# Token compression of a hybrid decoder step: cache pages laid by fours over the partitions, and turned in 32 x 32 blocks by VectorE

## What is computed

```python
CMP_BLOCK = 32; CMP_STRIDE = 16; CMP_HID = 256
def compress_rows(rows, pe, w1, w2):
    chunks = rows.reshape(B, nch, CMP_STRIDE, NSA_GROUPS, NSA_DK)
    w1r = w1.reshape(R, CMP_STRIDE, NSA_DK, CMP_HID)      # R = 2
    h = jnp.einsum('ld,ldh->h', pe, w1.reshape(CMP_BLOCK, NSA_DK, CMP_HID))
    for r in range(R):
        part = jnp.einsum('bcjgd,jdh->bcgh', chunks, w1r[r])
        h = h + part[:, r:r + nc]
    return jnp.einsum('bcgh,hd->bcgd', jax.nn.gelu(h), w2)
```

## Time and profile before

| | us |
|---|---|
| median of 3 runs | 1766.05 |
| lowest and highest | 1763.57, 1773.09 |
| the profiled execution | 1772.42 |
| its span | 1770.6 |
| compression stage in it | 413 to 681 |
| granted clock of TensorE, mean | 0.953 |

### The profile page before, as it was taken

How to read it: one execution, slowest core, us unless ns; L and a number is a source line. 1 busy time by engine, 2 the same in 40 slices (tenths; PEclk the granted TensorE clock), 3 DMA queues, 4 the chain that set the end, 5 groups by cost and what they waited for, 6 DMA issues and landing times. The chain is left out here.

```text
span 1770.6 us, 32705 instructions
## 1 busy us (share of the span) xinstructions
PE 1653.9 (93%) x12968; PEld 1374.8 (78%) x12968; DVE 804.5 (45%) x1873; ACT 585.9 (33%) x1235; POOL 105.8 (6%) x194
## 2 busy tenths in 40 slices
PE   6999999998799997789999989998979999999997
PEld 4888888776688885567677766766767999999997
DVE  4576543124233335866765643553554442234322
ACT  4232212222233234655554422332433331123210
POOL 0000000000000000034421200000010000000000
PEclk9999999999899998989897989999989999999999
DMA  8845545342533035531331089999752243333321
GB/s 276 296 163 165 157 160 164 97 131 57 139 72 77 7 98 153 138 137 58 109 110 36 7 315 369 363 371 346 278 177 72 95 129 113 113 113 124 96 71 51
DMA packets 187903, 265.71 MB, mean 150 GB/s; under 512 B 35261, under 2 KB 115517, under 8 KB 187654
## 3 DMA queue, kind: packets, MB, share of 16 engines
q1 hardware_dynamic: 183750, 244.31, 42.8%
q10 hardware_dynamic: 3136, 11.22, 1.7%
q0 software_dynamic: 896, 8.56, 1.5%
HBM read 240.98 MB, written 42.60 MB: 160 GB/s over the span
## 5 line engine op out<-in xcount | busy, mean ns | idle before, releaser
L620 PE MATMUL pj_ps<-all_hi,pj_xh 128*128 128x512 f32 x480 | 192.0, 400 | 1.5 <-DVE all_lo L509 1.5
L621 PE MATMUL pj_ps<-all_lo,pj_xh 128*128 128x512 f32 x480 | 190.0, 396 | 0.0
L622 PE MATMUL pj_ps<-all_hi,pj_xl 128*128 128x512 f32 x480 | 189.9, 396 | 0.0
L1431 ACT ACTIVATE pa_sc<-pa_sc,pa_nmax 128x32 f32<-128x32 f32 (+4 forms) x256 | 126.0, 493 | 124.9 <-DVE pa_nmax L1480 124.5
L2687 PE MATMUL fi_ps<-fi_fl,fi_wh 128*128 128x272 f32 x512 | 149.4, 292 | 0.0
L2688 PE MATMUL fi_ps<-fi_th,fi_wl 128*128 128x272 f32 x512 | 148.3, 290 | 0.0
L2688 PE MATMUL fi_ps<-fi_fh,fi_wl 128*128 128x272 f32 x512 | 148.3, 290 | 0.0
L2686 PE MATMUL fi_ps<-fi_th,fi_wh 128*128 128x272 f32 x512 | 147.6, 288 | 0.7 <-DVE fi_tl L2488 0.7
L2686 PE MATMUL fi_ps<-fi_fh,fi_wh 128*128 128x272 f32 x512 | 148.2, 290 | 0.0
L2687 PE MATMUL fi_ps<-fi_tl,fi_wh 128*128 128x272 f32 x512 | 147.2, 287 | 0.0
L2071 ACT ACTIVATE de_slot<-de_ps_t 128x512 f32<-128x512 f32 (+5 forms) x124 | 62.7, 513 | 174.8 <-PE de_ps_t L1905 85.3
(11 more groups left out here) (325 smaller groups left out, 3263.0 us busy)
## 6 DMA issues: line engine op xcount, KB each, us to landing
de_dv<-in_cache_diff SPq DMA_DIRECT2D x64, 512.0 KB, 10.1
all_big<-in_w_in SPq DMA_DIRECT2D x14, 2048.0 KB, 8.6
all_big<-in_cache_nsa SPq DMA_DIRECT2D x96, 256.0 KB, 5.9
de_dk<-in_cache_diff SPq DMA_DIRECT2D x48, 512.0 KB, 8.8
all_big<-in_w_up SPq DMA_DIRECT2D x16, 1024.0 KB, 5.5
all_big<-in_w_down SPq DMA_DIRECT2D x16, 1024.0 KB, 6.1
all_first<-in_cache_nsa SPq DMA_DIRECT2D x32, 256.0 KB
all_win<-in_cache_win SPq DMA_DIRECT2D x32, 256.0 KB, 7.2
```

Source lines behind the costliest of these rows:

```text
L620: pe.matmul(ps[:, t, :], xh[:, k, xk], hi(k), start=k == 0, stop=False)
L621: pe.matmul(ps[:, t, :], xh[:, k, xk], lo(k), start=False, stop=False)
L622: ins = pe.matmul(ps[:, t, :], xl[:, k, xk], hi(k), start=False, stop=k == KT - 1)
L1431: nc.scalar.activation(tile, tile, ACT.Exp, scale=-1.0, bias=nmax[:, x.n % 6, a:a + 1], accum_out=x.sums[a]).then_inc(probs, 1)
```

## The change

A quarter of the partitions now holds every fourth token. `page_load` issues four DMAs for a page, one for each remainder a of the token number by four: eight chunks of four tokens, to the partitions 32 a + 8 (i mod 4) + chunk, four tokens one behind the other at block i // 4 of the row. The rows of w1 and of the position embedding are laid in the matching order, each with eight DMAs of 32 partitions in place of one of 128. `lay_out` becomes two transposes on VectorE, each of 32 x 32 blocks over 128 partitions and 1024 elements, from the raw pages to `laid`, which is now in SBUF what `pt` was in PSUM. `high_parts` and `low_parts` read `laid`, in two pieces of 1024 elements in place of four of 512. TensorE's turns are gone. Chunks of one sequence now stand in order, so the second read of `xh` is one column on instead of 16, the copies behind the 128 columns are replaced by two columns of zeros set once, and a store is one DMA of 128 rows instead of eight.

```diff
-def page_load(nc, sp, g, d, dst, pair, i):
+def page_load(nc, sp, g, d, dst, pair, i, arrived):
 
     page = sp.value_load(g.table[0:1, PAGES_AT_ONCE * pair + i:PAGES_AT_ONCE * pair + i + 1],
                          min_val=0, max_val=d["cache_nsa"].shape[0] - 1)
-    chunks = d["cache_nsa"].rearrange("n (c j) e -> n c j e", j=CMP_STRIDE)
-    return sp.dma_start(dst[i:P:PAGES_AT_ONCE, :, :],
-                        chunks[bass.ds(page, 1), :, :, 0:2 * KVW].rearrange("n c j e -> (n c) j e"))
+    tokens = d["cache_nsa"].rearrange("n (c s a) e -> n a c s e", s=4, a=4)
+    block, at = divmod(i, 4)
+    for a in range(4):
+        rows = slice(32 * a + CHUNKS_PER_PAGE * at, 32 * a + CHUNKS_PER_PAGE * (at + 1))
+        sp.dma_start(dst[rows, 4 * block:4 * block + 4, :], tokens[bass.ds(page, 1), a, :, :, 0:2 * KVW]
+                     .rearrange("n c s e -> (n c) s e")).then_inc(arrived, 16)
+
+
+def turned_blocks(dst):
+
+    return dst.rearrange("p h g (b r) -> p b g h r", r=32)
...
-                    sp.dma_start(shared.big[:, 1 - k, :].rearrange("p (k n) -> p k n", n=CMP_HID),
-                                 d[f"cmp_w1_{'kv'[k]}"].rearrange("(k p) n -> p k n", p=P)).then_inc(shared.w1_in[k], 16)
+                    w1 = d[f"cmp_w1_{'kv'[k]}"].rearrange("(q a h i) n -> a h i q n", a=4, h=2, i=32)
+                    for a in range(4):
+                        for h in range(2):
+                            sp.dma_start(shared.big[32 * a:32 * a + 32, 1 - k, :].rearrange("p (q h n) -> p h q n", h=2, n=CMP_HID)
+                                         [:, h, :, :], w1[a, h, :, :, :]).then_inc(shared.w1_in[k], 16)
...
-            dve.wait_ge(shared.pages_in, 16 * PAGES_AT_ONCE)
-            first = shared.first[:].rearrange("p (j e) -> p j e", j=CMP_STRIDE)
-            nc.vector.tensor_copy(shared.laid[:].rearrange("p g (j e) -> p g j e", e=DK),
-                                  first[:, 0:JP, 0:KVW].rearrange("p j (g e) -> p g j e", e=DK)).then_inc(shared.laid_ahead, 1)
+            dve.wait_ge(shared.pages_in, 64 * PAGES_AT_ONCE)
+            first = shared.first[:].rearrange("p (b s e) -> p b s e", b=4, s=4)
+            for s2 in range(2):
+                nc.vector.transpose(turned_blocks(shared.laid[:, 2 * s2:2 * s2 + 2, :, :]), first[:, :, s2, 0:KVW]
+                                    ).then_inc(shared.laid_ahead, 1)
...
-GW = P + PAGES_AT_ONCE
+GW = P + 2
...
             def store(n):
                 sp.wait_ge(out_ready, n + 1)
                 if n < N_UNITS:
-                    i = PAGES_AT_ONCE * (n // 2)
-                    dst = d["kc_s" if n % 2 == 0 else "vc_s"].rearrange("(i c) e -> c i e", c=CHUNKS_PER_PAGE)
-                    for c in range(CHUNKS_PER_PAGE):
-                        sp.dma_start(dst[c, i:i + PAGES_AT_ONCE, :], out[PAGES_AT_ONCE * c:PAGES_AT_ONCE * (c + 1), n % 2, :]
-                                     ).then_inc(stored[n % 2], 16)
+                    at = P * (n // 2)
+                    sp.dma_start(d["kc_s" if n % 2 == 0 else "vc_s"][at:at + P, :], out[:, n % 2, :]).then_inc(stored[n % 2], 16)
...
-                sp.wait_ge(laid_out, 4 * (pair - 1))
+                sp.wait_ge(laid_out, 8 * (pair - 1))
                 load(pair)
                 store(2 * pair - 4)
                 store(2 * pair - 3)
-            sp.wait_ge(laid_out, 4 * (N_PAIRS - 1))
-            sp.dma_start(raw[0][0:CHP, :, :], nsa_p_chunks[:, :, 0:2 * KVW]).then_inc(raw_in[0], 16)
+            sp.wait_ge(laid_out, 8 * (N_PAIRS - 1))
+            for a in range(4):
+                sp.dma_start(raw[0][32 * a:32 * a + CHP, 0:4, :], nsa_p_tokens[a, :, :, 0:2 * KVW]).then_inc(raw_in[0], 16)
...
             def high_parts(v):
                 if v >= 2:
                     act.wait_ge(*half_read(v - 2))
-                for g in range(GROUPS):
-                    i = 4 * v + g
-                    act.wait_ge(turned, i + 1)
-                    nc.scalar.activation(xh[:, v % 2, :, g, 0:P], pt[:, i % 2, :].rearrange("p (j c) -> p j c", j=4),
-                                         ACT.Copy).then_inc(x_hi, 1)
-                act.wait_ge(x_hi, 4 * v + 4)
-                nc.scalar.activation(xh[:, v % 2, :, :, P:GW], xh[:, v % 2, :, :, 1:1 + PAGES_AT_ONCE].bitcast(F32),
-                                     ACT.Copy).then_inc(wrapped_hi, 1)
+                for s2 in range(2):
+                    js = slice(2 * s2, 2 * s2 + 2)
+                    act.wait_ge(laid_out, 2 * v + s2 + 1)
+                    nc.scalar.activation(xh[:, v % 2, js, :, 0:P], laid[v % 2][:, js, :, :], ACT.Copy).then_inc(x_hi, 1)
 
...
+                for x in (xh, xl):
+                    for u in range(2):
+                        nc.vector.memset(x[:, u, :, :, P:GW].bitcast(F32), 0.0).then_inc(behind, 1)
...
             def lay_out(v):
                 n, jh = divmod(v, 2)
                 pair, k = divmod(n, 2)
-                r, u = rows_of(n), pair % 2
                 if v >= 4 and k == 0 and jh == 0:
-                    dve.wait_ge(raw_in[u], RAW_LEVEL(pair) if n < N_UNITS else RAW_LEVEL(N_PAIRS - 2) + 16)
+                    dve.wait_ge(raw_in[pair % 2], RAW_LEVEL(pair))
                 if v >= 2:
-                    dve.wait_ge(turned, 4 * (v - 1) if v < HALVES + 2 else BANKS + v - HALVES - 1)
-                nc.vector.tensor_copy(laid[v % 2][0:r, :, :].rearrange("p g (j e) -> p g j e", e=DK),
-                                      raw[u][0:r, JP * jh:JP * (jh + 1), KVW * k:KVW * (k + 1)].rearrange("p j (g e) -> p g j e", e=DK)
-                                      ).then_inc(laid_out, 1)
-
-            dve.wait_ge(shared.laid_ahead, 1)
-            nc.vector.nop().then_inc(laid_out, 1)
+                    dve.wait_ge(x_hi, 2 * v - 2)
+                    dve.wait_ge(x_lo, 2 * v - 2)
+                src = raw[pair % 2].rearrange("p (b s) e -> p b s e", b=4)
+                for s2 in range(2):
+                    nc.vector.transpose(turned_blocks(laid[v % 2][:, 2 * s2:2 * s2 + 2, :, :]),
+                                        src[:, :, 2 * jh + s2, KVW * k:KVW * (k + 1)]).then_inc(laid_out, 1)
+
+            def lay_prompt(k):
+                if k == 0:
+                    dve.wait_ge(raw_in[0], RAW_LEVEL(N_PAIRS - 2) + 16 * 4)
+                dve.wait_ge(x_hi, LAID - 2 + 2 * k)
+                dve.wait_ge(x_lo, LAID - 2 + 2 * k)
+                nc.vector.transpose(laid_p[k].rearrange("p (s h) (g r) -> p s g h r", h=2, r=CHP),
+                                    raw[0][:, 0:4, KVW * k:KVW * (k + 1)]).then_inc(laid_out, 1)
+
+            dve.wait_ge(shared.laid_ahead, 2)
+            for s2 in range(2):
+                nc.vector.nop().then_inc(laid_out, 1)
             fill()
...
             def low_parts(v):
                 if v >= 2:
                     dve.wait_ge(*half_read(v - 2))
-                for g in range(GROUPS):
-                    i = 4 * v + g
-                    dve.wait_ge(x_hi, i + 1)
-                    nc.vector.tensor_tensor(xl[:, v % 2, :, g, 0:P], pt[:, i % 2, :].rearrange("p (j c) -> p j c", j=4),
-                                            xh[:, v % 2, :, g, 0:P].bitcast(F32), ALU.subtract).then_inc(x_lo, 1)
-                dve.wait_ge(x_lo, 4 * v + 4)
-                nc.vector.tensor_copy(xl[:, v % 2, :, :, P:GW], xl[:, v % 2, :, :, 1:1 + PAGES_AT_ONCE].bitcast(F32)
-                                      ).then_inc(wrapped_lo, 1)
+                for s2 in range(2):
+                    js = slice(2 * s2, 2 * s2 + 2)
+                    dve.wait_ge(x_hi, 2 * v + s2 + 1)
+                    nc.vector.tensor_tensor(xl[:, v % 2, js, :, 0:P], laid[v % 2][:, js, :, :],
+                                            xh[:, v % 2, js, :, 0:P].bitcast(F32), ALU.subtract).then_inc(x_lo, 1)
...
-            def turn(v, g):
-                if g == 0:
-                    pe.wait_ge(laid_out, v + 1)
-                i = 4 * v + g
-                if i >= 2:
-                    pe.wait_ge(x_lo, i - 1)
-                for j in range(4):
-                    ins = pe.transpose(pt[:, i % 2, P * j:P * (j + 1)], laid[v % 2][:, g, P * j:P * (j + 1)], ident[:])
-                ins.then_inc(turned, 1)
...
-                pe.wait_ge(wrapped_hi, v + 1)
-                pe.wait_ge(wrapped_lo, v + 1)
+                pe.wait_ge(x_lo, 2 * v + 2)
...
-                            at = slice(PAGES_AT_ONCE * half, PAGES_AT_ONCE * half + P)
+                            at = slice(half, half + P)
...
-                        if slot in TURN_SLOTS:
-                            x = TURN_SLOTS.index(slot)
-                            if v + 1 < HALVES:
-                                turn(v + 1, x)
-                            else:
-                                turn_prompt(x // 2, x % 2)
```

More of the change, by code:

```diff
@@ L741, in load @@
                 for i in PAGE_ORDER:
[L742 removed]
+                    page_load(nc, sp, shared, d, raw[pair % 2], pair, i, raw_in[pair % 2])
             def store(n):
```

(32 more changed lines are left out.)

54 lines of the change are left out of this document (22 added, 32 removed).

## The result

The changed kernel takes 1823.7 us (median of four runs, 1814.9 to 1831.0), the kernel before 1764.8 us on the same chip: a ratio of 1.032, with a 95% interval of 1.026 to 1.039. It is slower by some 59 us. The forecast was 1821 us.

A forecast was written before the change was run, and what follows sets the result against it. TensorE, busy 93%, was taken to bound the kernel, but after the change SyncE's page issue would set the compression's pace. The stage 55 us longer turned 1772.4 into 1827 us, or 1821 against the median of 1766; range 1762 to 1845.

The forecast's parts named there:

- the term that decides: SyncE's queue in the compression: four DMAs a page at 0.655 us each, 4.58 us a page, 73 us a pair.
- The start of load(1): Compression's start: VectorE and ScalarE no longer wait for turns, so load(1) starts at about 424.5 instead of 427.7 us.
- The holes and the end of the loops: TensorE in the compression: idle from about 456 to 505, 556 to 579, 630 to 653; loops end at 715.1 us.
- the sum: Compression: pair 3 issued by 645.5 us after 220 us for 48 pages, five halves follow, stage 55 us longer.
- The low clock: TensorE's lower granted clock after a long idle hole in the compression, put at 3.3 us.
- The gain on offer: Compression's main loops without turns, hole and low clock: 192 us, ending at 611.7 us, 48 us earlier.
- The rival: Compression: turns gone and pages landing in time, so pages no bound; loops end at 611.7, total 1718 us; chance 0.05.
- the lower bound: Page transfer into eight neighbouring partitions: 56 GB/s, 4.7 us a page, adding 5 us over three pairs, left in the range.
- the rule on ports: SBUF transfers: four neighbouring partitions share one of 16 ports at 27.2 GB/s; two ports would take 4.8 us a page.
- Small costs: VectorE's transpose of 1024 elements per partition at 1.1 us, 4.4 us a half, covered by TensorE's 11.1 us.
- no gaps between halves outside the holes: TensorE: no idle between halves in the projection, and no gaps in the compression's matmuls outside the three holes.

The follow-up runs named there:

- split4: The kernel before, with each page loaded by four DMAs instead of one, into the same partitions 16 apart, turns still on TensorE; 1832.9 us, ratio 1.042.
- spread4: The changed kernel, still four DMAs a page, but each quarter written to eight partitions 4 apart instead of eight neighbours; 1824.1 us, ratio 1.037.
- two_queues: The changed kernel, with pairs 1 to 3 issued by two engines: SyncE quarters 0 and 1 of each page, GpSimd 2 and 3; 1753.9 us, ratio 0.996.
- two_q_wait: two_q_low, with GpSimd waiting until SyncE's pages of the present pair have landed before issuing its pages of the next; 1718.2 us, ratio 0.972.
- two_q_low: The changed kernel, with one DMA a page into 32 partitions, low parts ahead of transposes, every second page of pairs 1 to 3 by GpSimd; 1728.2 us, ratio 0.979.

## Why the prediction was right

**The page's issue, the term that decides: right.** Forecast 4.58 us from page to page and 73 us a pair; measured 4.71 and 75.3, from the first issue for pair 1 to the first for pair 2 (427.39 to 502.67). The quarter took 0.674 us where I had taken 0.655, and the table read, in its median, 0.832 instead of 0.768. The choice of the page load itself as the nearest row was the step that mattered. With split4, spread4 and two_queues the cause is shown, not only argued.

**The start of load(1): 2.9 us too early.** It was at 427.39, not 424.5; from before (427.68) nothing was gained. VectorE's low part of w1 ended at 424.5, 1 us later than forecast, but the load also waits for TensorE's second set of position rows, which stand behind half 0's first low parts and six matmuls and ended near 426.3. They took 3.23 us, at a granted clock of 0.53, for 1.91 us at full clock before. I had looked at one of the two waits ahead of the load.

**The holes and the end of the loops: right in form, 7.8 us early.** Forecast 456 to 505, 556 to 579 and 630 to 653; measured 461.8 to 509.0, 560.7 to 584.4 and 635.9 to 660.8. The loops end at 722.9 instead of 715.1: 2.9 us for the start, 4.6 for the queue (225.6 us from the first issue to the end of the last, 221 in the sum), and 0.3 behind it. From the last hole to the end it took 62 us, as in the sum. The tail is 21.9 us in both kernels. The low clock came as forecast, behind each hole. Behind the first it was 0.50 and 0.57 in the first six us, then full:

```profile
509.00:512.00 3.00, 2.96 (x7) 2.39 (x8) 2.62 (x7) 2.43 (x4) 0.00 (x0) 0.50 0.24 67
512.00:515.00 3.00, 3.00 (x9) 2.33 (x9) 3.00 (x4) 0.95 (x1) 0.00 (x0) 0.57 0.14 49
515.00:518.00 3.00, 3.00 (x15) 2.39 (x14) 2.78 (x3) 0.00 (x0) 0.00 (x0) 1.00 0.20 57
```

**The total: right, with two errors that cancel.** Profile against profile, the stage is 63.2 us longer (744.7 against 681.5), 8 more than forecast; the span is only 46.7 us longer. The other 16.5 us lie behind the stage, most of them in the prompt's attention, whose code is the same. The prediction had nothing for that stretch; that the two errors cancel is luck. The profile of before granted less clock there; first its row, then that of after, at the same distance from the stage's end:

```profile
881.50:1021.50 140.00, 127.98 (x893) 104.52 (x893) 86.65 (x347) 68.22 (x253) 27.84 (x54) 0.86 0.16 49
...
944.70:1084.70 140.00, 123.49 (x1012) 100.87 (x1015) 90.72 (x365) 68.90 (x257) 27.81 (x54) 0.93 0.23 74
```

The profile of before was one of the longer runs of its kernel (1772.4 us against a median of 1766), which the prediction took into account with 6 of these 16 us. Between the medians of the result the change is 58.9 us, so there some 4 us of the stage's 63 come back.

What decides the clock behind the stage was not tried, but the thirteen profiles show a pattern. From the stage's end to that of the span, the five kernels whose stage ends at 735 us or later took 1070 to 1076 us, the eight others 1075 to 1089, before among the longest. The mean granted clock there was 0.953 to 0.961 in the five and 0.936 to 0.956 in the others. So part of the 16.5 us may belong to the change, since TensorE stood idle longest in those five; which part stays open.

**The gain on offer: right.** The sum had 48 us for turns, hole and clock, loops of 192 us, and 1718 us for pages that are no bound. two_q_wait has loops of 195.6 us, a stage that ends 47.5 us earlier than before, and 1718.2 us. By its loops the turns were worth 238.8 - 10.7 - 3.3 - 195.6 = 29.2 us, for which the sum had 28. The rival was right about the mechanism; in the changed kernel its condition isn't met by far.

**The transfer: the lower bound was put on the wrong kernel.** 56 GB/s is right for one DMA of a page into eight neighbours (55 measured), and so is the rule on ports that I weighed beside it. What I took from the same place, that a second DMA beside the first hardly helps, is not borne out for the DMAs of this case: two_queues moved 84 to 120 GB/s, and two_q_low 152 where one queue moved 102. For four quarters it was no bound: with two queues they moved 100 GB/s on average, in the changed kernel the DMA rate fell to between 2 and 26 GB/s once a page, and without neighbours (spread4) the pace was the same. As the issue stood at 4.71 us a page, this cost the forecast nothing; it had left that bound in the range alone.

**Small costs.** A transpose of 128 x 1024 on VectorE takes 1.22 us for my 1.1, and is covered: in two_q_wait TensorE has no idle time from 425 to 485 us. The projection with its 64 quarter loads and the sixteen DMAs for w1 shows TensorE busy for all of 100 to 345 us, as before. The forecast of no gaps between halves outside the holes held.

## What to carry over

A transfer that is split so that an engine can work on it has a price on the queue that issues it; count issues times their measured length against the time that the consumer leaves for them, before counting bytes. Then look at the same load's share, its longest issue, and the time from the last issue to the landing. In this case short issues, a low share and a landing 2 to 3 us behind the last issue went with the issue as the limit; drawn-out issues, or a landing 9 to 33 us behind, with the transfer. Often another order of rows gives the consumer the same layout with one DMA: here the stride of 4 within a block turned a loss of 3% into a gain of 1.4%, and of 2.8% with VectorE's new order and a second queue that doesn't run ahead.
